# Retention inside the projection: 32 units run piecewise between k steps, and GpSimd takes the norm's scale and shift

## The reference, cut to what matters

```python
h = rms_norm(x, pre_mix_g); proj = h @ w_in
r_q, r_k, r_v, r_g, a_q, a_c, i_q, i_k, i_w = split_cols(proj)
rq, rk = rotate(r_q, positions), rotate(r_k, positions)    # 8 heads of 64
# per head, in 8 chunks of 128 rows:
#   intra = (q_n k_n^T * decay) v_n;  cross = (q_n * xi) R_{n-1};  R_n = g^128 R_{n-1} + (k_n * zeta)^T v_n
ry = layer_norm(retention_chunkwise(rq, rk, rv), ret_norm_g, ret_norm_b)   # per head, over 64
y_ret = silu(r_g) * ry
# indexer: scores of 8 heads, top 256 keys of each row (exact, with ties); attention over them -> y_dsa
mix = concatenate([y_ret, y_dsa]) @ w_out
```

## Time and profile before

| | |
|---|---|
| median of 3 runs | 1430.29 us (1429.07 to 1430.95) |
| span of the profiled execution | 1428.3 us |
| the profiled execution's own time | not listed beside its span; the three runs above stand 0.8 to 2.7 us over the span |
| PE busy, PEld busy | 1376.4 us (96%), 1125.8 us (79%) |
| DVE, ACT, POOL busy | 1013.1 (71%), 605.1 (42%), 329.0 us (23%) |
| mean granted TensorE clock | 0.995 |
| DMA | 189.02 MB, mean 132 GB/s |

### The profile page before, as it was taken

One profiled execution on the slowest core, in us unless ns is written; L12 is line 12 of the kernel. 1 busy time (PEld: TensorE's weight loads), 2 busy tenths in 40 slices (PEclk: granted clock), 3 DMA queues, 4 the chain that ended last, 5 costly groups with the idle time before them and its releaser, 6 DMA issues.

```text
span 1428.3 us, 19391 instructions
## 1 busy us (share of the span) xinstructions
PE 1376.4 (96%) x7142; PEld 1125.8 (79%) x7142; DVE 1013.1 (71%) x1592; ACT 605.1 (42%) x1229; POOL 329.0 (23%) x383
## 2 busy tenths in 40 slices
PE   7999999999989889998999999999999999999998
PEld 7887888887777567777778888888887888888886
DVE  5748789998999546765877777777776765565633
ACT  6434552315823776574522222222222656453221
POOL 4545457711541475652000000000000000000000
PEclk9999999999999999999999999999999999999999
DMA  6322223225323021133234555444458866662211
GB/s 215 82 56 71 79 84 116 94 92 192 111 101 143 31 74 61 45 91 107 55 131 165 177 177 177 161 148 153 156 193 289 316 239 223 237 213 75 67 53 45
DMA packets 137150, 189.02 MB, mean 132 GB/s; under 512 B 12768, under 2 KB 75616, under 8 KB 137056
## 3 DMA queue, kind: packets, MB, share of 16 engines
q1 hardware_dynamic: 120224, 152.17, 32.5%
q10 hardware_dynamic: 16832, 35.61, 6.5%
HBM read 130.08 MB, written 57.67 MB: 131 GB/s over the span
## 4 chain that ended last, share of the span: by engine, by line
PE 79%; DVE 7%; issue 4%; ACT 4%; POOL 3%; DMA 1%; DVEq 1%; SPq 0%; ACTq 0%; POOLq 0%
PE ps L728 23%; PE ps L729 23%; PE ps L730 23%; PE ps L930 2%; PE ps L922 2%; PE ps L941 1%; PE ps L769 1%; POOL mxs L2721 1%; DMA raw<-in_w_in 1%; DVE sc L1915 1%; ACT lm L1444 1%; DVEq L1931 1%; PE ps L857 1%; PE ps L892 1%; PE ps L855 1%
## 5 line engine op out<-in xcount | busy, mean ns | idle before, releaser
L2593 POOL TENSOR_TENSOR smf<-smf,sml 128x1 f32<-128x1 f32 x16 | 9.1, 579 | 739.3 <-DVE smf L2474 625.2
L728 PE MATMUL ps<-bh,ah 128*128 128x512 f32 x308 | 120.1, 390 | 2.4 <-DVE u2b L2315 2.4
L730 PE MATMUL ps<-bh,al 128*128 128x512 f32 x308 | 119.9, 389 | 0.0
L729 PE MATMUL ps<-bl,ah 128*128 128x512 f32 x308 | 119.8, 389 | 0.0
L728 PE MATMUL ps<-wbh,xth 128*128 128x512 f32 (+1 forms) x320 | 118.9, 371 | 0.0
L729 PE MATMUL ps<-wbl,xth 128*128 128x512 f32 (+1 forms) x320 | 117.7, 368 | 0.0
L730 PE MATMUL ps<-wbh,xtl 128*128 128x512 f32 (+1 forms) x320 | 117.7, 368 | 0.0
L2421 DVE TENSOR_TENSOR al<-ra,ah 128x512 fp32r<-128x512 f32 x77 | 53.1, 690 | 70.7 <-ACT ah L1671 70.3
L728 PE MATMUL ps<-th,ssh 128*128 128x512 f32 x240 | 93.6, 390 | 1.8 <-DVE u2b L2291 1.2
L730 PE MATMUL ps<-th,ssl 128*128 128x512 f32 x240 | 93.4, 389 | 0.0
L729 PE MATMUL ps<-tl,ssh 128*128 128x512 f32 x240 | 93.4, 389 | 0.0
(11 more groups left out here) (375 smaller groups left out, 3871.1 us busy)
## 6 DMA issues: line engine op xcount, KB each, us to landing
raw<-in_w_in SPq DMA_DIRECT2D x49, 256.0 KB, 3.0
wt<-in_w_ffn_down SPq DMA_DIRECT2D x44, 256.0 KB, 7.2
down_sums<-wt ACTq DMA_DIRECT2D x44, 256.0 KB, 5.0
ra<-hidden_sums SPq DMA_DIRECT2D x44, 256.0 KB, 2.9
rb<-down_sums SPq DMA_DIRECT2D x44, 256.0 KB, 3.5
raws<-in_w_ffn_gate SPq DMA_DIRECT2D x21, 512.0 KB, 3.9
raws<-in_w_ffn_up SPq DMA_DIRECT2D x21, 512.0 KB, 5.3
ret_rows<-stg SPq DMA_DIRECT2D x32, 320.0 KB, 3.4
```

Source lines behind the costliest of these rows:

```text
L728: pe.matmul(o, ah, wh, start=start, stop=False, skip_group_check=resumes)
L729: pe.matmul(o, ah, wl, start=False, stop=False, skip_group_check=resumes)
L730: return pe.matmul(o, al, wh, start=False, stop=stop, skip_group_check=resumes)
```

## The change: what it does

The retention has no stage of its own any more. Its 96 parts stand between the k steps of units 32 to 55: four places in each unit of groups 4 and 5, five in each of group 6. Part q of this order is the pair bank of retention unit q/3, the scores of the one before or the output of the one before that, so that the three parts of one unit lie four places apart. The rows of each unit are loaded one by one (256 KB) into a ring of five. `keep_clock` goes from this stretch. The gate's silu is taken when the projection's bank is evacuated, and the gate is loaded on its own. The transposes of pairs 0 and 1 and of the latent (`CKV`) move into units 48 to 53, those of the last two pairs stay in the mix. On DVE the bits of the search are laid out anew around the norms (`BITS_BEFORE`: 24 bits up to the last pair's scale, 8 after it); scale and gate of a pair stay on DVE, gain and bias of pairs 0, 1 and 2 go to POOL, where roots, gains and low parts have fixed places by unit (`ROOT_AT`, `GAIN_AT`, `YR_LO_AT`), as do the low parts of the first two slices of `w_out`. The counts of block 4 write to SBUF and no longer to PSUM, and many buffers get other addresses.

```diff
-    AQ = sb("aq", [P, NP, S], 148)
+    AQ = sb("aq", [P, NP, S], 112)
...
+    JUNKS = {b: sb(f"junks{b}", [P, (b + 1) * P], a, mybir.dt.uint8) for b, a in ((4, 1.75), (5, 1.75), (6, 206.5), (7, 175))}
+    TIE_A, RANK_A = (sb(f"{n}_a", [P, (B0 + 3) * P], a, mybir.dt.bfloat16) for n, a in (("tie", 196.5), ("rank", 198)))
...
+    NRING = 5
+    RPR = [sb(f"rpr{i}", [P, 4 * P], 148 + 2 * i) for i in range(NRING)]
+    QKT = [sb(f"qkt{i}", [P, 256], 158 + i) for i in range(3)]
+    ST = [sb(f"st{i}", [P, 256], 161 + i) for i in range(2)]
+    RST = [sb(f"rst{i}", [P, P], 163 + 0.5 * i) for i in range(4)]
+    O = [sb(f"o{i}", [P, RT, P], a) for i, a in enumerate((165, 169, 192.5))]
+    SGR = [sb("sgr0", [P, RT, P], 196.5), sb("sgr1", [P, RT, P], 200.5)]
+    PT1 = sb("pt1", [P, RT, P], 196.5)
+    RGB = [sb(f"rgb{i}", [P, 2, P], 173 + i) for i in range(2)]
+    YRT = [sb(f"yrt{i}", [P, S], a) for i, a in enumerate((128, 132, 136))]
...
+    RET_AT = 4 * KT
+    RET_K, RET_K_LAST, RET_SKIP = (1, 3, 5, 7), (1, 2, 4, 5, 7), 2
+    RET_STEPS = len(RET_K) * 2 * KT - RET_SKIP + len(RET_K_LAST) * KT
+    PAIR_IN, SCORES, OUT = range(3)
+
+    def ret_step(g, k):
+
+        if g < RET_AT:
+            return None
+        if g < 6 * KT:
+            q = len(RET_K) * (g - RET_AT) + RET_K.index(k) - RET_SKIP if k in RET_K else -1
+        else:
+            q = len(RET_K) * 2 * KT - RET_SKIP + len(RET_K_LAST) * (g - 6 * KT) + RET_K_LAST.index(k) if k in RET_K_LAST else -1
+        what, n = q % 3, q // 3 - q % 3
+        return (what, n) if q >= 0 and 0 <= n < NP * RT else None
...
+    YR_AT = {(6 * KT, 3): (0, 0), (6 * KT, 6): (0, 1), (6 * KT + 4, 3): (1, 0), (6 * KT + 4, 6): (1, 1)}
+    CKV_AT = {(6 * KT + 5, 3): 0, (6 * KT + 5, 6): 1}
+    GATE_LOAD_AT = {44: 0, 48: 1, 53: 2, 54: 3}
+    WO_LOAD_AT = 6 * KT + 4
+    WO_HI_AT = {53: 0, 54: 1, 55: 2}
+    WO_POOL = 2
+    ROOT_AT = {42: 0, 47: 1, 53: 2}
+    GAIN_AT = {44: 0, 49: 1, 54: 2}
+    YR_LO_AT = {50: 0, 54: 1}
+    BITS_BEFORE = {("center", 0): 2, ("scale", 0): 3, ("gate", 0): 4, ("center", 1): 1, ("scale", 1): 3, ("gate", 1): 3,
+                   ("center", 2): 1, ("scale", 2): 3, ("gate", 2): 2, ("center", 3): 1, ("scale", 3): 1}
 
...
+        def load_pair(n):
+
+            hp, r = divmod(n, RT)
+            if n < NRING:
+                sp.wait_ge(s["t_ix"], ITEMS)
+            else:
+                sp.wait_ge(s["t_ro"], n - NRING + 1)
+            sp.wait_ge(st_ret[n % 2], 16 * (n // 2 + 1))
+            sp.dma_start(RPR[n % NRING][:, :], ret_dram[hp, r * P:(r + 1) * P, 0:4 * P]).then_inc(load_rp[n % NRING], 16)
+
...
+            for n in ret_loads(g):
+                load_pair(n)
+            if g == RET_AT + 1:
+                load_norm_gains(0)
+                load_norm_gains(1)
+            if g == WO_LOAD_AT:
+                load_out_weights()
+            if g in GATE_LOAD_AT:
+                load_gate(GATE_LOAD_AT[g])
+                if 1 <= GATE_LOAD_AT[g] < NP - 1:
+                    load_norm_gains(GATE_LOAD_AT[g] + 1)
+
...
+        def pair_bank(n):
+
+            hp, r = divmod(n, RT)
+            pe.wait_ge(load_rp[n % NRING], 16 * (n // NRING + 1))
+            if n == 0:
+                pe.wait_ge(s["v_acc"], ITEMS)
+            else:
+                pe.wait_ge(s["a_rb"], n)
+            rp, o = RPR[n % NRING], bank(2)
+            pe.transpose(o[:, 0:P], rp[:, 0:P], ID)
+            m = pe.transpose(o[:, P:2 * P], rp[:, P:2 * P], ID)
+            if r < RT - 1:
+                v01 = rp[:, RV:RV + 2 * P].rearrange("p (a c) -> p a c", c=HD)[:, 0:4:3, :]
+                m = pe.matmul(bank(6, P), rp[:, P:2 * P], v01, start=(r == 0), stop=True, skip_group_check=(r > 0))
+            m.then_inc(s["t_rb"], 1)
+
+        def scores(n):
+            pe.wait_ge(s["a_rb"], n + 1)
+            if n >= 1:
+                pe.wait_ge(s["a_st"], n)
+            qk = QKT[n % 3]
+            for h, j in enumerate(HALF):
+                m = pe.matmul(bank(4 + h, P), qk[j, P:2 * P], qk[j, 0:P], start=True, stop=True)
+            m.then_inc(s["t_sc"], 1)
+
+        def ret_out(n):
+            r = n % RT
+            pe.wait_ge(s["p_st"], n + 1)
+            if n >= 1:
+                pe.wait_ge(s["a_o"], n)
+            o = bank(7, P)
+            if r > 0:
+                pe.matmul(o, QKT[n % 3][:, 0:P], RST[n % 4][:, :], start=True, stop=False)
+            for h in range(2):
+                m = pe.matmul(o, ST[n % 2][:, h * P:(h + 1) * P], RPR[n % NRING][:, RV + h * P:RV + (h + 1) * P],
+                              start=(r == 0 and h == 0), stop=(h == 1))
+            m.then_inc(s["t_ro"], 1)
...
+        def retention_step(g, k):
+            if ret_step(g, k):
+                what, n = ret_step(g, k)
+                if what == PAIR_IN:
+                    pair_bank(n)
+                elif what == SCORES:
+                    scores(n)
+                else:
+                    ret_out(n)
+            if (g, k) in YR_AT:
+                output_transposes(*YR_AT[g, k])
+            if (g, k) in CKV_AT:
+                latent_transposes(CKV_AT[g, k])
...
+                retention_step(g, k)
...
-        pe.wait_ge(s["a_yrt"], NP - 2)
-        pe.wait_ge(s["a_rb"], NP * RT)
-        for r in range(RT):
-            m = pe.transpose(pair(0)[:, r * P:(r + 1) * P], CKV[:, r, :], ID)
-        m.then_inc(s["t_nt"], 1)
-        pe.wait_ge(s["a_o"], NP * RT)
-        keep_clock(6, 12)
-        pe.wait_ge(s["a_st"], NP * RT)
         retention_mix(0, (0, 1))
         retention_mix(1, (0, 1))
-        keep_clock(2, 8)
-        pair_outputs_transposes(NP - 2)
-        pe.wait_ge(s["a_yrt"], NP - 1)
+        for half in range(2):
+            output_transposes(NP - 2, half)
         retention_mix(2, (0, 1))
-        pe.wait_ge(s["a_nt"], 1)
-        pair_outputs_transposes(NP - 1)
         for b in range(3):
             retention_mix(b, (2,))
+        for half in range(2):
+            output_transposes(NP - 1, half)
         for b in range(3):
             retention_mix(b, (3,))
...
-                ins = sc.copy(STG[n % 2][:, RG_:RG_ + P], o[:, 3 * P:4 * P])
+                ins = sc.activation(STG[n % 2][:, RG_:RG_ + P], o[:, 3 * P:4 * P], ACT.Silu)
...
+            for k in range(KT):
+                read_retention_step(g, k)
             evacuate(g)
...
+            if g in WO_HI_AT:
+                out_weights_hi(WO_HI_AT[g])
...
+            bits(BITS_BEFORE["center", hp])
             ret_center(hp)
-            search_step(SEARCH_B, SIGN - BITS_AHEAD - hp, JUNKM)
-            if hp >= 1:
-                out_weights_lo(2 * hp - 2)
-                out_weights_lo(2 * hp - 1)
-            if hp == NP - 2:
-                ret_center(NP - 1)
-            for step in range(4):
-                ret_scale(hp, step)
-        for step in range(4):
-            ret_scale(NP - 1, step)
+            bits(BITS_BEFORE["scale", hp])
+            ret_scale(hp).then_inc(s["v_lnv"], 1)
+            bits(BITS_BEFORE["gate", hp])
+            ret_gate(hp)
+        out_weights_lo(2)
+        bits(BITS_BEFORE["center", NP - 1])
+        ret_center(NP - 1)
+        out_weights_lo(3)
+        bits(BITS_BEFORE["scale", NP - 1])
+        link(ret_scale(NP - 1))
+        ret_gain()
+        ret_gate(NP - 1)
...
+        def ret_gain(hp):
+
+            o, rows = O[hp % 3][:, :, :], RGB[hp % 2]
+            pool.wait_ge(s["load_retg"], max(64, 32 * (hp + 1)))
+            pool.wait_ge(s["v_lnv"], 2 * hp + 2)
+            link(g_.tensor_tensor(o, o, rows[:, 0, :].unsqueeze(1).to_broadcast([P, RT, P]), ALU.mult))
+            g_.tensor_tensor(o, o, rows[:, 1, :].unsqueeze(1).to_broadcast([P, RT, P]), ALU.add).then_inc(s["p_lnr"], 1)
+
...
+            for k in range(KT):
+                if ret_step(g, k) and ret_step(g, k)[0] == SCORES:
+                    causal_scores(ret_step(g, k)[1])
             if g + KT < LAST:
...
+            if g == RET_AT - 1:
+                pool.wait_ge(s["t_ix"], ITEMS)
+                for i in range(4):
+                    g_.memset(RST[i][:, :], 0.0).then_inc(s["p_zero"], 1)
+            if g in ROOT_AT:
+                ret_root(ROOT_AT[g])
+            if g in GAIN_AT:
+                ret_gain(GAIN_AT[g])
+            if g in YR_LO_AT:
+                ret_lo(YR_LO_AT[g])
+        for k in range(WO_POOL):
+            out_weights_lo(k)
+        ret_lo(NP - 2)
         ret_root(NP - 1)
```

More of the change, by code:

```diff
@@ new lines, in latent_transposes @@
+        def latent_transposes(half):
+            pe.wait_ge(s["v_nrm"], 3)
+            pe.wait_ge(s["a_yrt" if half == 0 else "a_nt"], 4 if half == 0 else 1)
+            for i in range(4):
+                m = pe.transpose(bank(3)[:, i * P:(i + 1) * P], CKV[:, 4 * half + i, :], ID)
+            m.then_inc(s["t_nt"], 1)
+        def retention_step(g, k):
[5 more added lines that the diff above has]
+                    scores(n)
+                else:
+                    ret_out(n)
```

(46 more changed lines are left out.)

431 lines of the change are left out of this document (157 added, 274 removed).

## The result

The changed kernel takes 1439.2 us (median of 4 runs, 1438.4 to 1439.9), the kernel before 1429.7 beside it (1429.1 to 1431.0). The ratio is 1.0060, 95% interval 1.0046 to 1.0075: slower by 9.5 us, where I had forecast 1421.6 us. The profiled execution took 1439.9 us, its span is 1438.2.

A forecast was written before the change was run, and what follows sets the result against it. PE and DVE both bound the attention (454.05 and 454.08 us). Projection's end 387.3, then the tail with its waits and 2.5 us of clock, put PE's leaving at 445.3: gain 8.7, median 1430.3 to 1421.6, range 1414 to 1430.

The forecast's parts named there:

- Waits inside the projection: none taken: PE in units 32 to 55: loads and copies come in time, no waits counted; cover thin only at unit 55.
- What a part costs: Retention parts on PE inside the projection: 1.73 us a unit, 52.8 us in all (47 to 70); projection ends at 387.3.
- The rival of the restart: Each of 96 parts interrupting the projection costs PE a restart; 0.18 us each gives 1438.9; chance 0.08 within 0.2%, 0.06 slower.
- The tail: From projection's end through the mix: PE idles 2.6, 2.1 and 4.5 us, leaves at 445.3; last bit 442.6.
- The wait for ACT's split: DVE in the tail, after gate 2 at 385.9: waits until ACT splits the third `w_out` slice at 389.2.
- The 2.5 us for the clock: PE in the mix after 4.5 us of idleness, without `keep_clock`: slower clock costs 2.5 us (0 to 5).
- 24 products: End of the mix on PE: first three blocks' last pair, with five whole blocks, 46 products of 0.68 us, 31.3.
- DVE up to pair 2: DVE's search and norms from 271.45 us: ten steps at 4.2 us, then at 372.5 a wait for pair 2's root until 375.8.
- The edits taken at nothing: Block 4's count to SBUF, mix gain-row loads, `w_out` low-half wait before mix stores, silu at evacuation: counted as nothing.
- The tables' rival: ACT in units 16 to 31 reloads tables for silu and relu at 1.28 us; up to 20 us, 1442; chance 0.02.
- a rival above: Follow-up with identity transposes in PE's tail: below 3 us of idle in one place the clock doesn't fall; 1420.5 to 1421.5.

The follow-up runs named there:

- early loads: Changed kernel with SyncE issuing the first five row loads of retention one unit earlier, ahead of that unit's weight load and row store: 1428.4 us, ratio 0.9982.
- merged parts: Against the kernel with early loads, PE does two neighbouring retention parts back to back, about 55 interruptions of the projection instead of 96: 1429.6 us, ratio 0.9990.
- The experiment with the roots: Changed kernel with only the square roots of pairs 0 and 2 one unit earlier in POOL's order (units 41 and 52): 1439.2 us, ratio 1.0063.

## Why the prediction was wrong

| | predicted | changed kernel | early loads |
|---|---|---|---|
| PE waits at unit 32 | 0 | 8.36 | 0 |
| projection ends | 387.3 | 402.3 | 390.5 |
| idle before mix, pair 2's products, pair 3's transposes | 2.6, 2.1, 4.5 | 2.2, 2.8, 4.1 | 2.2, 2.8, 4.1 |
| last gate ends, behind the projection's end | 22.3 | 24.5 | 24.5 |
| PE leaves the mix | 445.3 | 462.8 | 451.1 |
| last bit | 442.6 | 460.0 | 447.7 |

**The step that failed** is "Waits inside the projection: none taken". It said that a row load "has seven places of time", and the only wait of SP that it priced was the one for an output, which delays weights that are "needed eight units later". Both hold for the loads of the stream: no wait inside units 33 to 55 is in the trace. Neither covers the first one. It has no seven places: it may go when the indexer is done, at 201.3, and is wanted at 205.4, and it landed 3.8 us after its issue, not 3.0. And SP's wait for POOL delays not only the weights that it guards but all that is queued behind them: there the first load stood, with no unit of lead. It cost 8.4 us of idle and about 2 of half clock, and taking it away gave 10.8. I had counted what a wait in SP guards, not what stands behind it. A wait of PE inside units 32 to 54 was the prediction's own sign of a wrong mechanism, and it is there. The same step's sentence on the last unit, that PE isn't late at unit 55, held.

**What a part costs** was nearly right. Read as above, all parts of the kernel with early loads sum to 54.5 us, against 52.8: whole units take 1.75 to 1.77 us for 1.73 (a bank 0.45, scores 0.63, an output 0.68, where the old stage had 0.54, 0.42 and 0.77), and a bank without its addition or an output without its state product saves 0.22, not 0.33. The other products' matmuls, 370 of them, have a mean spacing of 0.231 us instead of 0.227, 1.5 us. These two are the mis-sized terms of this step, and the projection ends at 390.5, 3.2 us after the prediction; why the spacing grows no run shows. The rival of the restart had the right time for the wrong reason: 1438.9 against 1439.2. Its own sign, units longer by 1 us, is nowhere (the 24 units with early loads are 3.4 us longer in all), and merged parts gave nothing back.

**The tail** came as laid out: the same three waits, on the same engines, within 0.7 us each. It is 60.5 us long against 58.0, and 2.2 of the 2.5 lie ahead of the last gate, in two sizes on DVE. Two bits before gate 2 took 13.2 us (391.4 to 404.6) beside POOL's gain and low parts, not the 8.4 I gave them, so that the last centring began 8.4 us behind the projection's end and not 6.8. The centring itself took 6.3 us, not 5.3; one of its operations took 2.18 instead of 1.23 beside a low part of POOL. The wait for ACT's split, forecast near 386, isn't there, since gate 2 ended behind the split. The 2.5 us for the clock were right: 11 matmuls at 0.43 instead of 0.227 behind the last wait are 2.2. The eight ahead of it are paid out of the wait for the last gate. (The prediction's "24 products" for the last pair of three blocks are 6; its sum of 46 products has them as 6.)

**DVE up to pair 2** was off without harm. The search started near 263.5, not 271.5, so DVE met root 0 as well (12.3 us) and root 2 for 9.8 instead of 3.3. The experiment with the roots shows that this was slack. That the gains run at 2.4 us was right, for six operations of 2.39 to 2.40; that they cost DVE nothing beside bits was not.

**The edits taken at nothing** cost nothing that the trace shows. The stretch behind the mix is 1 us longer in the changed kernel and 1.5 with early loads, but in the twelve profiles it reads 973.5 to 978.9 us, and no experiment's edit touches it, so this is no finding. The tables' rival fell: one load with the first silu, 1283 ns, none after it in the projection.

```profile
90.02 1.28 ACT L1348 ACT_TABLE_LOAD   x1
```

**The sum closes.** From the predicted 1421.6: 10.8 for the first load, 3.2 for the projection, 2.5 for the tail and 1.0 behind it are 1439.1, against 1439.2 measured. The first term is a difference of two medians, the others are read from single traces, whose executions differ by a few us; that it closes to 0.1 is luck. Without the failed step the change would have brought about 2 us, not 8.7.

## What to carry to other kernels

When work is moved into a stream, price the first item apart from the steady state: find in the issuing queue what stands ahead of its load, and what that waits for. A wait in an in-order queue holds all behind it, not only the transfer that it protects; that order, with its times, stands in the trace of the kernel before. And a long wait on an engine is worth nothing until the next stations behind it are known: here three of them (root, gain, split) had to move together, and then the order of the last pair, before the time followed.

## What the runs showed of the hardware that I had not expected

DVE's search bits can stop for POOL. In the changed kernel `flip`, 128x3, took 2.40 us from 394.71 and ended with POOL's bias (394.69, 2.39 us); the one of the last bit, at 459.80, takes 0.17. The update of `cand` took 2.26 us up to 404.6, where POOL's low part ended:

```profile
394.69 2.39 POOL L2718 TENSOR_TENSOR o<-o,rgb 128x1024 f32<-128x1024 f32 x1
...
399.90 4.69 POOL L2722 TENSOR_TENSOR late_rows_r<-late_rows,late_rows_r 128x1024 fp32r<-128x1024 f32 x2
```

So the bit from 391.39 to 398.38 took 6.99 us where one alone takes 3.73. The counts beside them, 128x768 to 128x1024 of one input, kept their 1.01 to 1.28 us, and large operations with two inputs pay as well: with only the roots earlier, gate 2 took 2.23 us for 1.23, beside a low part of POOL (397.05). The Trainium skill (SBUF — State Buffer, SBUF: two separate sides) says that the pair of ports shared by the two engines is an exclusive lock held for a whole instruction, and that DVE takes it for operations with two SBUF inputs or in a mode that uses two ports. The trace agrees for `cand` and the gate, and shows a tiny operation waiting out a whole one of POOL; whether `flip`, with one input, ran in such a mode no run shows.

The clock after idle time on PE: 2.2 us before the mix left it at full speed; 2.8 before pair 2's products was followed by eight matmuls at half clock, 8.4 at unit 32 by some 5 us. But 2.25 in the kernel before was followed by seven, and with only the roots earlier 1.91 before the last pair's transposes by ten, so the length of one idle stretch alone doesn't tell it, and the 3 us that a rival above had supposed don't hold.
